# Down products two pieces behind, and the first two pieces of an FFN in narrow banks

## The reference

```python
def rmsnorm(x, g):
    xf = x.astype(jnp.float32)
    y = xf * lax.rsqrt(jnp.mean(xf * xf, axis=-1, keepdims=True) + EPS)
    return (y * g.astype(jnp.float32)).astype(x.dtype)

def swiglu_ffn(x, w_gu, w_down):
    gate, up = jnp.split(x @ w_gu, 2, axis=-1)
    return (jax.nn.silu(gate) * up) @ w_down

x = x + 0.5 * swiglu_ffn(rmsnorm(x, ffn1_norm[i]), ffn1_w_gu[i], ffn1_w_down[i])
```

## Time and profile before

| what | us |
|---|---|
| three runs | 2502.96, 2500.62, 2496.52 |
| median | 2500.62 |
| the profiled execution, its own time | 2498.21 |
| its span in the profile | 2496.4 |

### The profile page before, as it was taken

How to read it: one execution, slowest core, us unless ns; L and a number is a source line. 1 busy time by engine, 2 the same in 40 slices (tenths; PEclk the granted TensorE clock), 3 DMA queues, 4 the chain that set the end, 5 groups by cost and what they waited for, 6 DMA issues and landing times.

```text
span 2496.4 us, 33530 instructions
## 1 busy us (share of the span) xinstructions
PE 2301.1 (92%) x12236; PEld 1919.3 (77%) x12236; DVE 1694.0 (68%) x2947; ACT 1280.4 (51%) x2108; POOL 262.7 (11%) x146
## 2 busy tenths in 40 slices
PE   6998879999998999899899896989998999879998
PEld 5887857888887945688788775767886888767886
DVE  6875878778764344777777647538776877567775
ACT  5654645556552343555565554316554655236553
POOL 0003210000002200100100114201002001111001
PEclk9999989999998857999999997879999999889999
DMA  6552334545534310355355232014553553314552
GB/s 236 201 194 90 135 110 183 197 177 181 199 140 150 125 39 26 128 194 193 144 202 189 101 137 93 1 41 179 180 183 134 204 199 119 115 60 169 202 194 72
DMA packets 64654, 362.99 MB, mean 145 GB/s; under 512 B 7464, under 2 KB 8232, under 8 KB 32488
## 3 DMA queue, kind: packets, MB, share of 16 engines
q1 hardware_dynamic: 64064, 360.31, 40.0%
q10 hardware_dynamic: 296, 0.27, 0.0%
q0 software_dynamic: 128, 0.26, 0.0%
HBM read 359.76 MB, written 1.05 MB: 145 GB/s over the span
## 4 chain that ended last, share of the span: by engine, by line
PE 80%; DVE 13%; ACT 5%; issue 1%; DMA 1%; SPq 0%; DVEq 0%; ACTq 0%
PE ps L188 78%; ACT work L178 3%; DVE work L129 3%; DVE WL L118 2%; PE ps L193 2%; DVE small L129 2%; DVE work L118 1%; ACT XBt L178 1%; ACT WH L178 1%; DVE small L118 1%; DVE XBt L129 1%; DVE work L123 1%; DMA ring<-wts 1%; DVE small L141 1%; DVE work L125 0%
## 5 line engine op out<-in xcount | busy, mean ns | idle before, releaser
L188 PE MATMUL ps<-XBt,WH 128*128 128x512 f32 (+1 forms) x3936 | 1220.0, 371 | 41.0 <-DVE WL L118 16.7
L118 DVE TENSOR_TENSOR WL<-ring,WH 128x1024 fp32r<-128x1024 f32 x582 | 723.3, 1243 | 290.2 <-ACT WH L178 261.3
L188 PE MATMUL ps<-XBt,WL 128*128 128x256 f32 x3376 | 900.5, 284 | 1.6 <-DVE XBt L129 1.5
L178 ACT ACTIVATE WH<-ring 128x1024 fp32r<-128x1024 f32 x662 | 701.7, 1060 | 319.7 <-PE ps L188 258.3
L188 PEld LDWEIGHTS ps<-XBt,WH 128*128 128x128 f32 x3936 | 708.1, 194 | 154.0 <-DVE XBt L129 15.0
L188 PEld LDWEIGHTS ps<-XBt,WL 128*128 128x128 f32 x3376 | 650.3, 193 | 34.1 <-DVE XBt L129 3.9
L178 ACT ACTIVATE work<-ps 128x256 f32<-128x256 f32 (+5 forms) x511 | 212.5, 416 | 433.4 <-PE ps L188 400.8
L118 POOL TENSOR_TENSOR WL<-ring,WH 128x1024 fp32r<-128x1024 f32 x80 | 193.0, 2412 | 1887.7 <-DVE HLt L118 1265.1
L188 PE MATMUL ps<-WH,HHt 128*128 128x512 f32 x704 | 276.4, 393 | 3.5 <-DVE HLt L118 3.4
L188 PE MATMUL ps<-WL,HHt 128*128 128x512 f32 x704 | 274.2, 389 | 0.0
L188 PE MATMUL ps<-WH,HLt 128*128 128x512 f32 x704 | 271.5, 389 | 0.0
(11 more groups left out here) (105 smaller groups left out, 1404.2 us busy)
## 6 DMA issues: line engine op xcount, KB each, us to landing
ring<-wts SPq DMA_DIRECT2D x248, 1024.0 KB, 5.8
ring<-wts SPq DMA_DIRECT2D x180, 512.0 KB, 3.8
ring<-wts SPq DMA_DIRECT2D x1, 1152.0 KB, 5.1
ct<-cons SPq DMA_DIRECT2D x1, 1086.5 KB, 13.3
Xt<-x SPq DMA_DIRECT2D x4, 256.0 KB, 5.3
out<-Xt SPq DMA_DIRECT2D x1, 1024.0 KB, 4.0
ring<-wts SPq DMA_DIRECT2D x2, 256.0 KB, 2.6
ring<-wts SPq DMA_DIRECT2D x1, 288.0 KB, 2.8
```

The lines of the kernel that those rows point to most:

```text
L118: self.done(self.e and self.e.tensor_tensor(out, a, b, op), inc)
L178: self.done(self.e and self.e.activation(out, a, f, **kw), inc)
L188: inst = self.e and self.e.matmul(out, l, r, start=start, stop=stop)
```

## The change

- Down products stand two pieces behind: after gate and up of piece j come those of piece j-2; at the last piece they stand between gate and up.
- The first two pieces (`NARROW`) are unpaired: three matmuls of 256 columns into the first half of a bank, with nothing to copy and add; VectorE reads the bank in the product with RB and in the product H, and these give the bank back (`gm`, `h`).
- No low part of an FFN weight is made on GpSimd. VectorE has them all, in a new order: gate and up of piece 1 ahead of the token scales, and the down part of a piece in its own step, where before it came a step earlier.
- `row_pe` stands in the middle of the up product of piece 1 and writes to the bank of the accumulator acc11, so that the down products wait for its copy.
- In `unscaled` one more square is taken ahead of the second half of the transposed copies.
- In nsa and od `row_pe` stands behind the second weight piece, and GpSimd waits for DG ahead of its low parts.

```diff
@@ -13,6 +13,7 @@
 NFF = 22
+NARROW = 2
 SLOT = 3072
@@ -320,9 +321,6 @@
         def on_pool(name, part):
-            if COLS[name] == 3072 and name[0] in "fg":
-                t, j = name.rsplit(".", 1)
-                return t != "f1.0" and (j, part) in (("0", 2), ("1", 0), ("1", 1))
             return part == 1 and COLS[name] == 2048 and name not in ROPE
@@ -534,16 +532,19 @@
             def act(A, between=None):
+                def square(half, i):
+                    A.wait_ge(f"{prev}.x{i}{half}")
+                    A.act(SQ4[:, half, i, :], X[:, i, half * 512:half * 512 + 512], ACT.Square,
+                          accum_out=n_s4[:, 2 * half + i:2 * half + i + 1], inc=f"{t}.sq" if half and i else None)
+
                 flip_act(A, t, g, 0)
-                for half in range(2):
-                    for i in range(2):
-                        A.wait_ge(f"{prev}.x{i}{half}")
-                        A.act(SQ4[:, half, i, :], X[:, i, half * 512:half * 512 + 512], ACT.Square,
-                              accum_out=n_s4[:, 2 * half + i:2 * half + i + 1], inc=f"{t}.sq" if half and i else None)
-                    if not half and between:
-                        between(A)
-                    if not half:
-                        flip_act(A, t, g, 1)
+                square(0, 0)
+                square(0, 1)
+                if between:
+                    between(A)
+                square(1, 0)
+                flip_act(A, t, g, 1)
+                square(1, 1)
 
@@ -558,15 +559,17 @@
 
-        def row_pe(P, t):
-            ps.take(f"{t}.rb")
-            P.wait_ge(f"{t}.dg", *ps.free(f"{t}.rb"))
-            P.mm(ps[f"{t}.rb"][:, 0:256], ONES, DG, True, True, inc=f"{t}.rb")
-            ps.give(f"{t}.rb", f"{t}.rbe")
-
-        def row_dve(V, t):
+        def row_pe(P, t, use=None):
+
+            bank = use or ps.take(f"{t}.rb")
+            P.wait_ge(f"{t}.dg", *ps.free(bank))
+            P.mm(ps[bank][:, 0:256], ONES, DG, True, True, inc=f"{t}.rb")
+            if use is None:
+                ps.give(bank, f"{t}.rbe")
+
+        def row_dve(V, t, use=None):
             V.wait_ge(f"{t}.rb")
-            V.cp(RB, ps[f"{t}.rb"][:, 0:256], inc=f"{t}.rbe")
+            V.cp(RB, ps[use or f"{t}.rb"][:, 0:256], inc=f"{t}.rbe")
 
@@ -637,7 +640,7 @@
                 wh, wl = wide(piece)
-                P.wait_ge(f"{t}.hl{j}", f"{piece}:lo2", *ps.free(f"{t}.acc{i}{n}"))
+                P.wait_ge(f"{t}.hl{j}", f"{piece}:lo2", *ps.free(f"{t}.acc{i}{n}"), f"{t}.rbe")
                 ws = slice(2048 + n * 512, 2560 + n * 512)
@@ -663,6 +666,10 @@
                     ws = slice(u * 1024 + kt * 128, u * 1024 + kt * 128 + 128)
+                    if j < NARROW:
+                        P.mm3(ps[use][:, 0:256], wh[:, ws], wl[:, ws], XH[:, kt, :], XL[:, kt, :], kt == 0, kt == 7,
+                              inc=f"{piece}:{'gu'[u]}" if kt == 7 else None)
+                        continue
                     if kt:
@@ -678,25 +685,26 @@
                             P.wait_ge(f"{t}.{j}:lo{u}", *ps.free(f"{t}.{'gu'[u]}{j}"))
-                            if j == 1 and u == 0:
+                            if j == 1 and u == 1:
                                 product(P, j, u, range(4))
-                                row_pe(P, t)
+                                row_pe(P, t, f"{t}.acc11")
                                 product(P, j, u, range(4, 8))
...
                                 product(P, j, u, kts)
+                            if j == NFF - 1 and u == 0:
+                                for n in range(2):
+                                    for i in range(2):
+                                        down(P, j - 2, n, i)
                         if j == 0 and kts[0] == 0:
...
                     for u in range(2):
-                        ps.give(f"{t}.{'gu'[u]}{j}", f"{t}.{'gu'[u]}{j}.e")
-                    if j == 0:
-                        for use in ("acc00", "acc10", "acc01"):
-                            ps.take(f"{t}.{use}")
-                    if j == 1:
-                        ps.take(f"{t}.acc11")
-                    if 0 < j < NFF - 1:
-                        for n in range(2):
-                            for i in range(2):
-                                down(P, j - 1, n, i)
+                        ps.give(f"{t}.{'gu'[u]}{j}", f"{t}.{('gm', 'h')[u]}{j}" if j < NARROW else f"{t}.{'gu'[u]}{j}.e")
+                    for n in range(2):
+                        for i in range(2):
+                            if j == 0:
+                                ps.take(f"{t}.acc{i}{n}")
+                            if 2 <= j < NFF - 1:
+                                down(P, j - 2, n, i)
                 for n, i in ((0, 0), (0, 1), (1, 0)):
@@ -711,29 +719,28 @@
                 hi(A, f"{t}.0", (0, 1))
-                norm.act(A, lambda A: hi(A, f"{t}.0"))
+                norm.act(A)
                 hi(A, f"{t}.1", (0, 1))
                 for j in range(NFF):
-                    nx1, nx2, b = ahead(f"{t}.{j}", 1), ahead(f"{t}.{j}"), j % 2
-                    hi(A, nx1, (0, 1))
-                    A.wait_ge(f"{t}.{j}:g")
-                    A.act(LW[:, b, 0:256], ps[f"{t}.g{j}"][:, 256:512], ACT.Copy, inc=f"{t}.gl{j}")
-                    if j < NFF - 1:
-                        hi(A, nx2, (0,))
+                    nx2, b = ahead(f"{t}.{j}"), j % 2
+                    if j >= NARROW:
+                        A.wait_ge(f"{t}.{j}:g")
+                        A.act(LW[:, b, 0:256], ps[f"{t}.g{j}"][:, 256:512], ACT.Copy, inc=f"{t}.gl{j}")
+                    hi(A, nx2, (0,) if j else (0, 1))
                     A.wait_ge(f"{t}.gm{j}")
                     A.act(TH[:, b, :], GU[:, b, 0:256], ACT.Tanh, scale=0.5, inc=f"{t}.th{j}")
-                    hi(A, nx2, (0,))
-                    A.wait_ge(f"{t}.{j}:u")
+                    hi(A, f"{t}.{j}", (2,))
+                    if j >= NARROW:
+                        A.wait_ge(f"{t}.{j}:u")
+                        A.act(LW[:, b, 256:512], ps[f"{t}.u{j}"][:, 256:512], ACT.Copy, inc=f"{t}.ul{j}")
                     if j < NFF - 1:
-                        A.act(LW[:, b, 256:512], ps[f"{t}.u{j}"][:, 256:512], ACT.Copy, inc=f"{t}.ul{j}")
                         hi(A, nx2, (1,))
+                    if j < NFF - 1:
                         A.wait_ge(f"{t}.h{j}")
...
                         A.act(HH[:, b, :], H[:, b, :], ACT.Copy, inc=f"{t}.hh{j}")
-                        hi(A, nx1, (2,))
                     else:
-                        A.act(LW[:, b, 256:512], ps[f"{t}.u{j}"][:, 256:512], ACT.Copy, inc=f"{t}.ul{j}")
                         for i in range(2):
@@ -746,32 +753,35 @@
                     if q == 3:
-                        lo(V, f"{t}.1", (0,))
+                        lo(V, f"{t}.1", (0, 1))
                 for j in range(NFF):
-                    nx1, nx2, b = ahead(f"{t}.{j}", 1), ahead(f"{t}.{j}"), j % 2
-                    if j:
-                        lo(V, nx1, (0, 1))
-                    V.wait_ge(f"{t}.gl{j}")
-                    V.tt(GU[:, b, 0:256], ps[f"{t}.g{j}"][:, 0:256], LW[:, b, 0:256], ADD, inc=f"{t}.g{j}.e")
+                    nx2, b = ahead(f"{t}.{j}"), j % 2
                     if j == 0:
-                        lo(V, nx1, (1,))
-                        row_dve(V, t)
-                    V.tt(GU[:, b, 0:256], GU[:, b, 0:256], RB, MUL, inc=f"{t}.gm{j}")
-                    if 0 < j < NFF - 1:
                         lo(V, nx2, (0,))
-                    if j == 0:
-                        lo(V, f"{t}.0")
+                        row_dve(V, t, f"{t}.acc11")
+                    if j < NARROW:
+                        V.wait_ge(f"{t}.{j}:g")
+                        V.tt(GU[:, b, 0:256], ps[f"{t}.g{j}"][:, 0:256], RB, MUL, inc=f"{t}.gm{j}")
+                    else:
+                        V.wait_ge(f"{t}.gl{j}")
+                        V.tt(GU[:, b, 0:256], ps[f"{t}.g{j}"][:, 0:256], LW[:, b, 0:256], ADD, inc=f"{t}.g{j}.e")
+                        V.tt(GU[:, b, 0:256], GU[:, b, 0:256], RB, MUL, inc=f"{t}.gm{j}")
+                    if j < NFF - 1:
+                        lo(V, nx2, (0,) if j else (1,))
                     V.wait_ge(f"{t}.th{j}")
                     V.stt(SG[:, b, :], TH[:, b, :], 1.0, GU[:, b, 0:256], ADD, MUL)
+                    lo(V, f"{t}.{j}", (2,))
                     if j < NFF - 1:
-                        V.wait_ge(f"{t}.ul{j}")
-                        V.tt(GU[:, b, 256:512], ps[f"{t}.u{j}"][:, 0:256], LW[:, b, 256:512], ADD, inc=f"{t}.u{j}.e")
-                        V.tt(H[:, b, :], SG[:, b, :], GU[:, b, 256:512], MUL, inc=f"{t}.h{j}")
-                        lo(V, nx2, (0, 1) if j else (0,))
+                        if j < NARROW:
+                            V.wait_ge(f"{t}.{j}:u")
+                            V.tt(H[:, b, :], SG[:, b, :], ps[f"{t}.u{j}"][:, 0:256], MUL, inc=f"{t}.h{j}")
+                        else:
```

(11 more changed lines are left out.)

3 lines of the change are left out of this document (2 added, 1 removed).

## The result

| | median us | runs |
|---|---|---|
| before | 2498.68 | 2496.52 to 2502.96 (4) |
| changed | 2454.81 | 2453.42 to 2457.18 (4) |

The ratio is 0.9823, with a 95% interval of 0.9806 to 0.9840: 43.9 us faster. The forecast was 2446 us, from a sum of 53.9 us of gain; the time lies within the range and the sign is right, with 10 us less gain than foretold. The profiled execution of the changed kernel took 2457.18 us, its span is 2455.4, which is 41.0 under the span of before.

The account below looks back on a forecast made before the run. TensorE, busy 92%, was the bound, with idle time at FFN and mixer starts. Gains 32.5 + 1.0 + 4.4 + 16.0 = 53.9 us gave 2444.3, against the median 2446.7, taken as 2446; range 2436 to 2470.

Parts of the forecast that it names:

- f2.0, g2.0, g1.1, g2.1: Four of five late FFNs: first down product earlier, a gain of 6.5 us in each.
- f1.1 and g1.0: FFNs where GpSimd had split early: a gain of 0.5 us each, first down product at F + 15.1.
- f1.0: FFN without GpSimd splits: 4.0 us from an earlier first down product plus 0.4 of a late second piece, 4.4.
- nsa and od: Mixers: token-scale product behind the second weight piece removes 4.98 us of idle and slow work, 8.0 us each, 16.0 together.
- Narrow pieces: First two pieces of each FFN: triples cost 0.4 us an FFN, 3.3 in all, sparing VectorE additions and ScalarE copies.
- No FFN splits on GpSimd: FFN starts: 21 splits go to VectorE at 1.23 us each, so its small operations are no longer blocked.
- both waits: TensorE's idle 1.96 us and 3.80 us at the start of f2.0, a pattern in five FFNs; both were to go.
- Down two behind: FFN start: gate and up of piece 2, 5.54 us, run before the first down product; late FFNs gain 6.5 us each.
- A late one delays only ScalarE: Steady pieces: a late weight load for piece j+4 holds up only ScalarE, costing nothing.
- rival (d): Steady pieces: a ring of waits doesn't close in 8.31 us, each of 160 pieces stalls; 2526 us at 0.5 each, chance 0.03.
- rival (a): FFN start: VectorE becomes the bound, seven FFNs lose up to 3.7 us; 2472 us, or half, 2459; chance 0.13.
- Rival (b): Mixers: their 16 us are waited for later, at another VectorE stage or weight load; 2462 us, chance 0.10.

Follow-up runs that it names:

- The repetition: The changed kernel timed once more without an edit: 2453.40 us, ratio 0.9821 against the kernel before.

## Why the prediction was right, and where not

The table gives each term beside what the profile shows.

| term | foretold us | measured us |
|---|---|---|
| f2.0, g2.0, g1.1, g2.1 | 26.0 | 25.3 |
| f2.1 | 6.5 | -0.2 |
| f1.1 and g1.0 | 1.0 | -0.4 |
| f1.0 | 4.4 | 4.1 |
| nsa and od | 16.0 | 16.7 |
| ev and ab | 0 | -4.9 |
| all the rest | 0 | 0.4 |

*Narrow pieces and the FFN start.* The time of the late FFNs came out 5.7 to 7.2 against 6.5, with the small waits where my timeline had them. But I gave a part of the gain to the wrong cause. "No FFN splits on GpSimd" was to take away both waits. With the splits back on GpSimd the late FFNs lose 0.2 us (g1.1 3.1), and without them the kernel before gains nothing in the sum of its FFNs. What takes the waits away is the later place of the token-scale product (15.2 us by the medians when undone) and, above all, the second step of delay (52.4 us when undone). With that, the chain from the scales through H to HL has room. Its last operation in f2.0, on VectorE,

```profile
380.73 0.42 DVE L119 TENSOR_TENSOR HLt<-work,HHt 128x256 fp32r<-128x256 f32 x1 [0.48 <-ACT HHt L179]
```

ends at F + 14.3, and TensorE comes to the first down product at F + 16.4; one step earlier it would stand at F + 9.7. The two are not additive, since each hides what the other leaves. The second step of delay was not tried alone on the kernel before, and the moved square not at all, so what each is worth by itself isn't shown.

*Down two behind, the steady pieces.* "A late one delays only ScalarE" is the step that failed. It is true for pieces 2 to 20, whose steps stayed 8.31 us, and rival (d) did not come. At piece 21 there is no later piece: ScalarE's 4.64 us in f2.1 went straight to TensorE and cost 5.97 us, shown by moving one conversion. I had worked ScalarE's order out for the middle of an FFN, and passed over a line of the diff that changes it at the end.

*f1.1 and g1.0.* I took 0.5 us of gain each; f1.1 gained 0.1 and g1.0 lost 0.5. Their first down product came at F + 15.7, not 15.1, and with GpSimd's splits back it is at F + 15.0: the three splits on VectorE cost 0.7 us there, which I had counted as hidden. This is the small part of rival (a) that came true.

*Mixers.* That 16.7 stands beside 16.0 is in part luck: the start of nsa gives 7.2 us, so two such starts 14.4, and the rest of the two stages varies by more than the difference, as above; in the means over all profiled executions the new order is worth 11.7 us. The third weight piece of nsa starts 7.2 us earlier against the end of f1.1 than before (14.92 against 22.13), not 8.0. VectorE's and GpSimd's splits beside it:

```profile
749.73 3.46 DVE L119 TENSOR_TENSOR WL<-ring,WH 128x1024 fp32r<-128x1024 f32 x1
```

```profile
749.71 2.40 POOL L119 TENSOR_TENSOR WL<-ring,WH 128x1024 fp32r<-128x1024 f32 x1 [2.78 <-DVE work L124]
```

VectorE's split of 1.23 us takes 3.46 and ends at 753.19, 0.06 us before TensorE goes on at 753.25. The token-scale product begins at 752.38 and takes 0.24 us where nothing behind it waits (374.55 to 374.79 in f2.0), so 0.63 of the missing 0.8 us is this wait, for which I had only a sentence beside the sum. By the lock rule of the Trainium skill (SBUF — State Buffer, "SBUF: two separate sides") the later operation waits for the whole of the other, 2.40 + 1.23 = 3.63 from 749.71; the trace agrees within 0.2 us. That the gain was passed on is shown by the mixers' part alone, 17.6 us. Undoing it in the changed kernel costs only 8.3: the profile shows the same waits at the start and another clock behind them, and what sets that clock was not tried.

*Rest.* Rival (b) looked half true in the first profile, since ev and ab took back 4.9 us. The repetition gave the same program another ev, 3.4 us shorter, so nothing was taken back by a wait.

## What to carry to other kernels

When a pipeline is delayed by one more step, check its last step apart from its steady ones: there an in-order engine that asks for the next stage's data ahead of this stage's last work has no later step to hide the wait, and a guard such as "not in the last step" may be there for that. A cause that is plain in the trace (GpSimd blocking VectorE) need not be the one to mend; moving the consumer back made it harmless in four of the five late FFNs. Where part of a kernel varies with the clock, compare the sum of the stages that TensorE fills: two executions of one program agreed within 0.1 us in that sum here, and differed by 3 us in the rest. A single kernel with a part undone then says little of a stage that varies; several kernels with and without the part say more.

## What the runs showed of the hardware

The granted clock falls also where TensorE has no idle time in the record. In nsa of the kernel before it is 1.00, then 0.50, with TensorE busy for all of each stretch:

```profile
827.67:830.17 2.50, 2.50 (x28) 2.39 (x26) 1.18 (x3) 0.00 (x0) 1.23 (x1) 1.00 0.38 56
...
831.50:832.00 0.50, 0.50 (x4) 0.50 (x3) 0.00 (x0) 0.00 (x0) 0.00 (x0) 0.50 1.08 459
...
835.17:837.67 2.50, 2.50 (x19) 2.50 (x18) 2.06 (x3) 0.25 (x2) 2.36 (x1) 0.50 1.02 429
```

What runs there are many small matmuls, of 64 columns when the clock falls, and of 15 after that (TensorE's timeline):

```profile
827.16 5.12 PE L188 MATMUL ps<-ring,work 128*15 128x64 f32 x48
832.21 8.15 PE L188 MATMUL ps<-work 64*128 64x15 f32 x46
```

So busy time in the record, whose ends are modelled, doesn't tell that the clock will stay up. How long it stays low there differs between kernels with the same work. Over the fourteen profiled executions ev, whose work no edit touched, took 281.3 us (clock 0.85) to 289.7 us (clock 0.82).

An idle stretch of TensorE can cost more than its length, and the surplus isn't fixed. Within one execution, a wait of 2.51 or 2.52 us moved the first down product by 1.5 us in f1.0, where the granted clock stayed at 1.00, by 3.0 in f2.0 and by 5.1 in g1.1, where it was 0.50 for 6 us. A wait of 4.65 us was followed by a step that was 1.6 to 2.8 us too long.
